# Finer waits in the feed-forward stage and a shorter way from the router into the experts

## The chip, the cores and the metric

The kernel runs on one core of a Trainium2 chip. The metric is the device time in microseconds (us) from the start to the end of one execution. The engines of the core are named as in its profile: PE is the matrix engine (PEld its weight loads), DVE the vector engine, ACT the scalar engine, POOL the GpSimd engine, SP the engine that issues most of the DMAs. Each works through its own list of instructions in order, and semaphores order them against each other.

## What is computed

The program is a stack of blocks over 512 tokens of width 1024, all in float32: a gated delta rule mixer, a SwiGLU feed-forward layer, a state space (S5) mixer, a mixture of experts and two attention layers, each with a residual and a layer norm. Two pieces matter here.

```python
def swiglu(x, w1, w3, w2):
    return (jax.nn.silu(x @ w1) * (x @ w3)) @ w2
...
    logits = (xt @ w_router).astype(jnp.float32) + b_router.astype(jnp.float32)
    top_v, top_i = lax.top_k(logits, TOP_K)
    gates = jax.nn.softmax(top_v, axis=-1)
    dense_gate = jnp.sum(jax.nn.one_hot(top_i, N_EXPERTS, dtype=jnp.float32) * gates[..., None], axis=1)
    y = jnp.zeros_like(xt)
    for e in range(N_EXPERTS):
        y = y + dense_gate[:, e:e + 1].astype(x.dtype) * swiglu(xt, w1[e], w3[e], w2[e])
```

The feed-forward layer has 2816 hidden features, the mixture eight experts (two per token) with 1408 each.

## The kernel before

**Three passes.** A float32 product is made of three products of rounded operands: high times high, low times high, high times low (`three_pass`). ACT writes the high part of a weight tile (`split_hi`, `ffn_w_hi`), DVE the low part as raw minus high (`split_lo`, `ffn_w_lo`), and only then may PE use it (`take`). The low part overwrites nothing that PE still reads: three tiles are held (`SPLITS`), and ACT waits with tile j until PE has entered tile j-2 (`tile_used`, `leave`).

**The feed-forward stage** (`dense_parts` with `beside` and `end` set) runs two parts of 1408 hidden features. A part has 18 tiles: 12 up tiles (six chunks, for each the w1 and the w3 tile, 1 MB each and 0.5 MB in the last chunk) and 6 down tiles. The eight PSUM banks serve the up products in a turn of four; then `keep_busy` (L194) puts six matmuls on a constant, then the down products accumulate in all eight banks. `keep_busy` computes nothing that is used. DVE multiplies gate and value (`ffn_prod`, L2710), POOL splits the product (`hid_hi`, `hid_lo`), and after the last down tile DVE adds the banks to `acc`.

**What runs beside it.** `Parameters` prepares later stages on DVE meanwhile. `condition` (L1896) multiplies two 128x1024 blocks of `ada_t` after each low part; SP loads two more blocks after each low part and before the next weight tile (`loads`, L1753). `output_powers` (L1879 to L1884) makes a group of powers, waits first for the store of the group before (L1769), and SP stores the group before it issues the next weight tile. In the first part the last two groups are computed one after the other, between the low parts of the second and the third down tile.

**The end of the stage.** The last three down tiles of the second part are gone through token block by token block (four of 128), with both halves of 512 columns in turn under each tile, so that `EndNorm` can add, measure (L2548), aggregate, centre and scale a block on DVE while PE does the next one. `turn` transposes the block.

**The router** (`router`, stage `s5_glu`) makes the layer norm, stores the rows of `x_tok` to DRAM, computes the logits, takes the two best experts, and counts with matrices of ones the place of each token within its expert (L3305) and the load of each expert (L3309). The flag `moe_fits` says whether all experts have at most 192 tokens.

**Into the experts** (`sparse_parts`). All engines load the flag and branch. SP loads the small table of slot numbers (L3159) and the first weight tiles (L2449). DVE compares the table with the places (`make_pick`), PE turns the picks into row numbers (`spots`, L2844), DVE reads them out (`read_spots`), POOL gathers the rows by an indirect DMA (L3052), PE transposes them (`turn`, L2852 and L2854), ACT and DVE write their high and low parts (`x_hi`, `x_lo`), and the first expert's up products begin (L2870). `keep_busy` stands three times in between:

```python
        keep_busy(prog, 6, 6)
        pe.wait_ge(token_ready, 1)
        spots(0)
        keep_busy(prog, 6, 12)
        turn(0)
        keep_busy(prog, 6, 4)
```

One `keep_busy` call is two records of PE in the trace. All eight experts then run in a loop.

## Time and profile before

| | |
|---|---|
| median of 3 runs | 2688.17 us (2687.33 to 2690.44) |
| profiled execution | 2686.12 us |
| its span, first to last instruction | 2684.4 us |
| mean granted clock of PE | 0.986 of full |
| PE busy | 2537.4 us, 95% |
| DVE, ACT, POOL busy | 64%, 38%, 20% |
| feed-forward stage in the trace | about 470 to 862 us |
| router and way into the experts | about 1060 to 1143 us |
| experts | about 1143 to 1780 us |

Times in the rows are from the start of the span. A busy PE can be a PE that works on `keep_busy`. An engine's idle time costs only where PE waits at its end.

### The profile page before, as it was taken

Reading aid. Unit: us, or ns where it says so; the run is one execution under the profiler, and the core shown is the slowest. Engines: PE = TensorE matmul, PEld = TensorE weight load, DVE = VectorE, ACT = ScalarE, POOL = GpSimd, SP = SyncE. Lnnn points to the kernel's source line nnn. Section 1 sums busy time; section 2 is a strip of 40 time slices with the busy share of each in tenths; the row PEclk is TensorE's granted clock in tenths of the full one; section 3 lists DMA queues with packets and bytes.
Section 4 is the critical chain, followed back from the end, with each engine's and each line's share of the span. In section 5 each row is a group of like instructions: output and inputs, shape, how many; then the busy total and the mean of one; then the engine's idle time right before and its main releaser. Section 6 shows DMA issues by size and latency. Waiting matters only on the chain. (4 is left out here: it accounts for less than half of the span.)

```text
span 2684.4 us, 42100 instructions
## 1 busy us (share of the span) xinstructions
PE 2537.4 (95%) x16443; PEld 2086.8 (78%) x16443; DVE 1720.3 (64%) x2855; ACT 1032.3 (38%) x1472; POOL 543.6 (20%) x429
## 2 busy tenths in 40 slices
PE   8998989999999989899999999989998989999897
PEld 7887887778877769799999999967675666776466
DVE  6745666466676783566666667665775546677456
ACT  3341213321212342355555555513343443344353
POOL 1104431430320110143233344320110001020001
PEclk9999999999999999999999999999999989999999
DMA  4221001346653342367777777743220212322021
GB/s 149 92 82 33 2 3 63 121 156 228 201 185 131 108 125 80 108 215 236 232 256 238 232 236 251 263 150 90 70 90 27 85 56 71 97 77 72 26 79 63
DMA packets 262242, 340.82 MB, mean 127 GB/s; under 512 B 24960, under 2 KB 220032, under 8 KB 261504
## 3 DMA queue, kind: packets, MB, share of 16 engines
q1 hardware_dynamic: 253888, 315.52, 36.6%
q0 software_dynamic: 4736, 16.78, 1.8%
q10 hardware_dynamic: 3456, 6.29, 0.8%
q8 instruction: 110, 1.80, 0.3%
q14 instruction: 52, 0.43, 0.1%
HBM read 318.63 MB, written 17.30 MB: 125 GB/s over the span
## 5 line engine op out<-in xcount | busy, mean ns | idle before, releaser
L2870 PE MATMUL ps<-x_feat_r,moe_w_hi 128*128 128x384 f32 x1408 | 405.1, 359 | 1.0 <-DVE x_feat_r L2970 1.0
L2476 DVE TENSOR_TENSOR moe_w_lo<-ring,moe_w_hi 128x2048 fp32r<-128x2048 f32 x144 | 314.5, 2184 | 117.7 <-ACT moe_w_hi L2471 117.5
L2873 PE MATMUL ps<-x_feat_r,moe_w_lo 128*128 128x192 f32 x1408 | 354.5, 252 | 0.0
L2471 ACT ACTIVATE moe_w_hi<-ring 128x2048 fp32r<-128x2048 f32 x144 | 255.0, 1771 | 99.3 <-PE ps L263 72.8
L2873 PEld LDWEIGHTS ps<-x_feat_r,moe_w_lo 128*128 128x128 f32 x1408 | 268.8, 191 | 0.3
L2870 PEld LDWEIGHTS ps<-x_feat_r,moe_w_hi 128*128 128x128 f32 x1408 | 264.2, 188 | 1.9 <-issue 1.6
L267 PE MATMUL ps<-x_free_r,ring_r 128*128 128x512 f32 x496 | 196.5, 396 | 0.0
L266 PE MATMUL ps<-ring_r,x_feat_r 128*128 128x256 f32 (+2 forms) x576 | 186.3, 323 | 0.0
L194 PE MATMUL ps<-cst 128*128 128x384 f32 x370 | 135.8, 519 | 19.6 <-PEq L175 17.3
L263 PE MATMUL ps<-x_feat_r,ffn_w_hi 128*128 128x512 f32 x352 | 139.3, 396 | 0.7 <-DVE ffn_w_lo L2476 0.7
L267 PE MATMUL ps<-x_feat_r,ffn_w_lo 128*128 128x512 f32 x352 | 139.4, 396 | 0.0
L266 PE MATMUL ps<-x_free_r,ffn_w_hi 128*128 128x512 f32 x352 | 138.5, 393 | 0.0
L2471 ACT ACTIVATE ffn_w_hi<-ring 128x2048 fp32r<-128x2048 f32 (+1 forms) x36 | 63.6, 1772 | 179.4 <-PE ps L263 136.0
L194 PEld LDWEIGHTS ps<-cst 128*128 128x128 f32 x370 | 72.1, 202 | 68.8 <-issue 30.8
L3778 ACT ACTIVATE s_sb<-s_sb,att_small 128x512 f32<-128x512 f32 (+3 forms) x128 | 71.8, 561 | 139.7 <-DVE att_small L3770 139.3
L266 PEld LDWEIGHTS ps<-ring_r,x_feat_r 128*128 128x128 f32 x576 | 110.8, 192 | 8.7 <-issue 0.6
L267 PEld LDWEIGHTS ps<-x_free_r,ring_r 128*128 128x128 f32 x496 | 93.6, 189 | 21.1
L3767 DVE CUSTOM_DVE_ANT_0 s_sb<-ps,tables 128x128 f32<-128x128 f32 (+3 forms) x104 | 49.3, 474 | 91.1 <-PE ps L3717 74.0
L3785 ACT ACTIVATE p_t<-ps 128x512 f32<-128x512 f32 (+3 forms) x128 | 55.0, 430 | 130.5 <-PE ps L3717 130.4
L263 PE MATMUL ps<-x_feat_r,acc_r 128*128 128x512 f32 x256 | 102.0, 398 | 0.0
L2917 ACT ACTIVATE moe_cross<-ps 128x384 f32<-128x384 f32 (+1 forms) x96 | 44.3, 462 | 146.8 <-PE ps L2873 146.8
L266 PE MATMUL ps<-x_free_r,acc_r 128*128 128x512 f32 x256 | 100.6, 393 | 0.0
(615 smaller groups left out, 6454.4 us busy)
## 6 DMA issues: line engine op xcount, KB each, us to landing
ring<-in_moe_w SPq DMA_DIRECT2D x120, 1024.0 KB, 5.5
ring<-in_w_in SPq DMA_DIRECT2D x32, 1024.0 KB, 5.3
ring<-in_ffn_w SPq DMA_DIRECT2D x30, 1024.0 KB, 7.0
ring<-in_ada_t SPq DMA_DIRECT2D x48, 512.0 KB, 4.1
ring<-in_gdn_w_in SPq DMA_DIRECT2D x12, 1024.0 KB, 5.7
ring<-in_moe_w SPq DMA_DIRECT2D x24, 512.0 KB, 3.8
ring<-in_s_w_glu SPq DMA_DIRECT2D x8, 1024.0 KB, 5.4
ring<-in_w_out SPq DMA_DIRECT2D x8, 1024.0 KB, 6.3
```

What stands on the lines that cost most here:

```text
L194: prog.nc.tensor.matmul(prog.ps[:, bank, 0:3 * P], prog.ident, prog.cst, start=True, stop=True)
L263: m = nc.tensor.matmul(out, lh, rh, start=first, stop=False)
L266: nc.tensor.matmul(out, lh, rl, start=False, stop=False)
L267: return nc.tensor.matmul(out, ll, rh, start=False, stop=last)
L2471: self.prog.nc.scalar.activation(self.flat(self.hi, j % SPLITS, j), self.raw(j), ACT.Copy).then_inc(self.hi_done, 1)
L2476: self.prog.nc.vector.tensor_tensor(self.flat(self.lo, j % SPLITS, j), self.raw(j), self.flat(self.hi, j % SPLITS, j).bitcast(F32), ALU.su ...
L2870: mm = nc.tensor.matmul(out, wh[:, k, cs], both[:, k, :], start=(k == 0), stop=False)
L2873: mm = nc.tensor.matmul(out[:, 0:SLOTS], wl[:, k, cs], xg[0][:, k, :], start=False, stop=(k == KD - 1))
L2917: nc.scalar.activation(cross_of(c, which), half(c, which, 1), ACT.Copy).then_inc(cross_copied, 1)
L3767: self.nc.vector.tensor_tensor_reduce(out=x, in0=scores, in1=table, scale=1.0, scalar=-3.0e38, op0=ALU.add, op1=ALU.max, accum_out=mx).the ...
L3778: self.nc.scalar.activation(x, x, ACT.Exp, bias=self.small[:, u % 4, 1:2], scale=self.heads[h][3], accum_out=self.small[:, u % 4, 2:3]).th ...
L3785: self.nc.scalar.activation(self.p_t[:, u % 2, 0:self.keys(u)], self.ps[:, 2 + u % 2, 0:self.keys(u)], ACT.Copy).then_inc(self.pt_copied, 1)
```

## The change

In the feed-forward stage: the first weight tile is rounded and split in four pieces, and PE waits for each piece of two k-steps rather than for the tile; `keep_busy` at the start goes from 8 to 2 calls. Between up and down the six `keep_busy` calls are gone, and the first down tile runs in an order of banks that follows when each comes free. The low part of the third down tile is computed between the two last groups of powers instead of behind both. In the token-by-token end each half of 512 columns is finished before the other begins, and its statistics are taken directly after its addition.

Between router and experts: the ranks are computed with four matmuls (32, 24, 16 and 8 columns) instead of ten, the loads with one instead of four, followed by one more reduction; the subtraction of 1 from the places is moved into the table. The slot table and the first three tiles of the first expert are loaded in the router stage (`first_expert_tiles`, after the stores of the rows); SP signals them in the expert stage. `keep_busy` before the spots goes from 6 to 2 calls. ACT rounds two tiles before the rows instead of one, DVE splits the first tile before `find_homes` and the second before the rows.

```diff
@@ class PartStream @@
+        self.first_hi, self.first_lo = None, None
+
+    def in_pieces(self, st):
+        self.first_hi, self.first_lo = st.counter("first_hi"), st.counter("first_lo")
+
+    def piece(self, p):
+        k, n = tile_rows(0)
+        return slice(p * k * n // PIECES, (p + 1) * k * n // PIECES)
+
+    def first_pieces_hi(self, act):
+        act.wait_ge(self.landed[0], 16)
+        act.wait_ge(self.tile_used, 1)
+        for p in range(PIECES):
+            cs = self.piece(p)
+            self.prog.nc.scalar.activation(self.hi[:, 0, cs], self.raw(0)[:, cs], ACT.Copy
+                                           ).then_inc(self.first_hi if p < PIECES - 1 else self.hi_done, 1)
+
+    def first_pieces_lo(self, dve):
+        for p in range(PIECES):
+            cs = self.piece(p)
+            if p < PIECES - 1:
+                dve.wait_ge(self.first_hi, p + 1)
+            else:
+                dve.wait_ge(self.hi_done, 1)
+            self.prog.nc.vector.tensor_tensor(self.lo[:, 0, cs], self.raw(0)[:, cs], self.hi[:, 0, cs].bitcast(F32), ALU.subtract
+                                              ).then_inc(self.first_lo if p < PIECES - 1 else self.lo_done, 1)
...
     def loads(self, sp):
 
         for j in range(RAW):
-            self.load(sp, 0, j)
+            sp.wait_ge(self.prog.expert_landed[j], 16)
+            sp.sem_inc(self.landed[j], 16)
...
+def first_expert_tiles(prog, sp, stage, inp):
+
+    W = prog.weights
+    for j in range(RAW):
+        c0, c1 = CHUNKS[j // 2]
+        src = inp[("moe_w1", "moe_w3")[j % 2]][0][0][:, c0:c1].rearrange("(k p) n -> p k n", p=P)
+        last_there = W.size[stage] - RING + j
+        sp.wait_ge(W.used, W.released[W.first[stage] + last_there])
+        sp.dma_start(W.ring[:, j, 0:KD * (c1 - c0)].rearrange("p (k n) -> p k n", n=c1 - c0), src
+                     ).then_inc(prog.expert_landed[j], 16)
...
@@ class EndNorm @@
-    def spread(self, dve, t, added, count):
+    def half_stats(self, dve, t, h, added, count):
+        dve.wait_ge(added, count)
+        self.nc.vector.bn_stats(self.stats[:, t, 6 * h:6 * h + 6], self.acc[:, t, h * BANK:(h + 1) * BANK]
+                                ).then_inc(self.measured, 1)
+
+    def spread(self, dve, t):
         self.link = self.link or linker(dve, self.norm_link)
-        dve.wait_ge(added, count)
-        for h in range(2):
-            m = self.nc.vector.bn_stats(self.stats[:, t, 6 * h:6 * h + 6], self.acc[:, t, h * BANK:(h + 1) * BANK])
-        self.link(m)
+        dve.wait_ge(self.measured, 2 * t + 2)
...
+FREED = (((5, 7), 0), ((0, 1, 2, 3), FT + 3), ((4, 6), FT + 4))
...
@@ dense_parts, tensor @@
         if beside:
-            keep_busy(prog, 7, 8)
+            keep_busy(prog, 7, 2)
...
                     for k in range(KD):
+                        if opening and m == 0 and k % (KD // PIECES) == 0:
+                            S_.first_piece(pe, k)
...
-            if beside:
-                keep_busy(prog, 5, 6)
-            pe.wait_ge(mult_done, e * FT + (FT + 4))
+            if not beside:
+                pe.wait_ge(mult_done, e * FT + (FT + 4))
...
                 wh, wl = S_.take(pe, e, j)
+                if beside and j == N_UP:
+                    pe.wait_ge(hid_ready, e * FT + 4)
+                    for banks, multiplied in FREED:
+                        if multiplied:
+                            pe.wait_ge(mult_done, e * FT + multiplied)
+                        for i in banks:
+                            t, cs = slice((i // 2) * P, (i // 2 + 1) * P), slice((i % 2) * BANK, (i % 2 + 1) * BANK)
+                            for m in range(2):
+                                three_pass(nc, ps[:, i, :], (hid_hi[:, m, t], hid_lo[:, m, t]), (wh[:, m, cs], wl[:, m, cs]),
+                                           m == 0, False, S_.leave if m == 0 and i == FREED[0][0][0] else None)
+                    continue
...
                 for t in range(NT):
-                    for j in range(N_TILES - by_token.TILES, N_TILES):
-                        if j not in held:
-                            held[j] = S_.take(pe, e, j)
-                        wh, wl = held[j]
-                        for r in range(tile_rows(j)[0]):
-                            m = 2 * (j - N_UP) + r
-                            pe.wait_ge(hid_ready, e * FT + (m + 3))
-                            for h in range(2):
-                                cs = slice(h * BANK, (h + 1) * BANK)
+                    for h in range(2):
+                        cs = slice(h * BANK, (h + 1) * BANK)
+                        for j in range(N_TILES - by_token.TILES, N_TILES):
+                            if j not in held:
+                                held[j] = S_.take(pe, e, j)
+                            wh, wl = held[j]
+                            for r in range(tile_rows(j)[0]):
+                                m = 2 * (j - N_UP) + r
+                                pe.wait_ge(hid_ready, e * FT + (m + 3))
...
@@ dense_parts, vector @@
                 if beside and c == LAST:
                     beside.vector(dve, e, LAST - 1)
-                    beside.vector(dve, e, LAST)
-            for j in range(N_UP + 2, N_TILES):
+            split_lo(e, N_UP + 2)
+            if beside:
+                beside.vector(dve, e, LAST)
+            for j in range(N_UP + 3, N_TILES):
                 split_lo(e, j)
...
@@ sparse_parts @@
-        keep_busy(prog, 6, 6)
+        keep_busy(prog, 6, 2)
         pe.wait_ge(token_ready, 1)
         spots(0)
         keep_busy(prog, 6, 12)
...
         S_.split_hi(act, 0, 0)
+        S_.split_hi(act, 0, 1)
         x_hi(0)
-        S_.split_hi(act, 0, 1)
...
-        dve.wait_ge(table_landed, 16)
+        dve.wait_ge(prog.slots_landed, 16)
         make_pick(0)
         nc.vector.tensor_copy(token.rearrange("p t n -> p (t n)"), token_id).then_inc(token_ready, 1)
         read_spots(0)
+        S_.split_lo(dve, 0, 0)
         low_gate = find_homes()
-        S_.split_lo(dve, 0, 0)
+        S_.split_lo(dve, 0, 1)
         x_lo(0)
-        S_.split_lo(dve, 0, 1)
...
@@ router @@
                 sp.dma_start(gb[:, :, :], inp["ln_gb"][2]).then_inc(landed, 16)
+                sp.dma_start(table, prog.slot_table).then_inc(prog.slots_landed, 16)
...
                 for t in range(NT):
                     sp.wait_ge(normed, t + 1)
                     sp.dma_start(prog.x_rows[t * P:(t + 1) * P, :], x_tok[:, t, :]).then_inc(stored, 16)
+                first_expert_tiles(prog, sp, "s5_glu", inp)
                 sp.wait_ge(stored, 16 * NT)
...
                 pe.wait_ge(chosen, 1)
-                for t in range(NT):
-                    for b in range(t + 1):
-                        m = nc.tensor.matmul(ps[:, 5, t * EXPERTS:(t + 1) * EXPERTS], prog.tri if b == t else prog.ones,
-                                             left[:, b, 0:EXPERTS], start=(b == 0), stop=(b == t))
+                nc.tensor.matmul(ps[:, 5, 0:NT * EXPERTS], prog.tri, left[:, :, 0:EXPERTS], start=True, stop=False)
+                for b in range(1, NT):
+                    m = nc.tensor.matmul(ps[:, 5, b * EXPERTS:NT * EXPERTS], prog.ones, left[:, 0:NT - b, 0:EXPERTS],
+                                         start=False, stop=(b == NT - 1))
                 m.then_inc(ranked, 1)
-                for t in range(NT):
-                    m = nc.tensor.matmul(ps[:, 7, 0:EXPERTS], prog.ones, left[:, t, 0:EXPERTS], start=(t == 0), stop=(t == NT - 1))
-                m.then_inc(ranked, 1)
+                nc.tensor.matmul(ps[:, 7, 0:NT * EXPERTS], prog.ones, left[:, :, 0:EXPERTS], start=True, stop=True
+                                 ).then_inc(ranked, 1)
...
-                dve.wait_ge(ranked, 2)
-                link(nc.vector.memset(place[:, :, EXPERTS:], -1.0))
-                pl = place[:, :, 0:EXPERTS]
-                link(nc.vector.tensor_tensor(pl, ps[:, 5, 0:NT * EXPERTS].rearrange("p (t n) -> p t n", n=EXPERTS),
-                                             left[:, :, 0:EXPERTS], ALU.mult))
-                link(nc.vector.tensor_scalar(pl, pl, 1.0, None, ALU.subtract))
-                link(nc.vector.tensor_reduce(den[:, 0:1], ps[:, 7, 0:EXPERTS], AX_X, ALU.max))
+                nc.vector.memset(place[:, :, EXPERTS:], 0.0)
+                dve.wait_ge(ranked, 1)
+                nc.vector.tensor_tensor(place[:, :, 0:EXPERTS], ps[:, 5, 0:NT * EXPERTS].rearrange("p (t n) -> p t n", n=EXPERTS),
+                                        left[:, :, 0:EXPERTS], ALU.mult)
+                dve.wait_ge(ranked, 2)
+                link(nc.vector.tensor_reduce(top[:, 0, 0:EXPERTS], ps[:, 7, 0:NT * EXPERTS].rearrange("p (t n) -> p n t", n=EXPERTS),
+                                             AX_X, ALU.add))
+                link(nc.vector.tensor_reduce(den[:, 0:1], top[:, 0, 0:EXPERTS], AX_X, ALU.max))
                 nc.vector.tensor_scalar(flag[:, :], den[:, 0:1], SLOTS + 0.5, None, ALU.is_lt)
```

`first_piece` is the wait of PE for one piece. In the constants, the slot numbers of the table go from 0, 1, ... to 1, 2, ..., and the first rows of the experts are one less. Both new sets of semaphores live outside the stages.

## Rows read from the trace of the kernel before

**Rows 1.** Windows: us, PE, PEld, DVE, ACT, POOL busy, granted clock, DMA share, GB/s

```profile
663.00:787.00 124.00, 124.00 (x535) 99.92 (x534) 85.43 (x94) 27.21 (x23) 36.49 (x20) 1.00 0.59 193
...
1143.00:1780.00 637.00, 633.66 (x3889) 588.50 (x3890) 427.89 (x370) 341.29 (x329) 230.64 (x179) 1.00 0.72 233
```

**Rows 2.** Waits of PE over the feed-forward stage: total us, times, longest

```profile
PE ps L263 <- DVE ffn_w_lo L2476: 0.7, 1, 0.7
```

**Rows 3.** Timeline of the stage's opening: start us, us, engine, line, out<-in, [idle before <- releaser]

```profile
469.91 5.40 PE L194 MATMUL ps<-cst 128*128 128x384 f32 x16 [0.55 <-PEq L175]
...
471.10 5.51 ACT L2471 ACTIVATE ffn_w_hi<-ring 128x2048 fp32r<-128x2048 f32 x3 [2.35 <-SPq L2766]
...
473.04 8.97 DVE L2476 TENSOR_TENSOR ffn_w_lo<-ring,ffn_w_hi 128x2048 fp32r<-128x2048 f32 x3 [3.46 <-ACT ffn_w_hi L2471]
...
475.99 0.50 PE L263 MATMUL ps<-x_feat_r,ffn_w_hi 128*128 128x512 f32 x1 [0.68 <-DVE ffn_w_lo L2476]
```

**Rows 4.** The low parts of the opening by source line: ns min/median/max

```profile
L2476 DVE TENSOR_TENSOR ffn_w_lo<-ring,ffn_w_hi x3: 2890/3119/3120, 473.0 to 478.9; 128x2048 fp32r<-128x2048 f32 x3
```

**Rows 5.** Window of the opening's gap, columns as in rows 1

```profile
475.00:476.00 1.00, 0.32 (x2) 0.01 (x1) 1.00 (x2) 1.00 (x1) 1.00 (x2) 1.00 0.00 0
```

**Rows 6.** Timeline of PE between up and down, first part

```profile
599.18 4.03 PE L194 MATMUL ps<-cst 128*128 128x384 f32 x12
602.76 0.68 PE L263 MATMUL ps<-ffn_w_hi,ffn_hid_hi 128*128 128x512 f32 x1
603.28 0.40 PE L266 MATMUL ps<-ffn_w_lo,ffn_hid_hi 128*128 128x512 f32 x1
```

**Rows 7.** Timeline of DVE in the first part's down phase

```profile
616.87 0.76 DVE L1879 TENSOR_TENSOR x_tok<-x_tok,s_pow 128x576 f32<-128x576 f32 x1 [3.71 <-DMA s_q<-x_tok]
...
621.26 2.29 DVE L2476 TENSOR_TENSOR ffn_w_lo<-ring,ffn_w_hi 128x2048 fp32r<-128x2048 f32 x1
...
625.75 2.29 DVE L2476 TENSOR_TENSOR ffn_w_lo<-ring,ffn_w_hi 128x2048 fp32r<-128x2048 f32 x1
```

**Rows 8.** Timeline of SP, the two blocks issued before the third down tile's successor

```profile
614.47 1.48 SPq L1753 DMA_DIRECT2D ring<-in_ada_t  x2
```

**Rows 9.** Those two blocks by tensor: time from issue to landing

```profile
DMA to landing us min/median/max: 7.0/7.8/8.7
```

**Rows 10.** Timelines of ACT and DVE, last down tile of the stage

```profile
825.20 1.06 ACT L2471 ACTIVATE ffn_w_hi<-ring 128x1024 fp32r<-128x1024 f32 x1 [9.27 <-PE ps L263]
...
826.30 1.23 DVE L2476 TENSOR_TENSOR ffn_w_lo<-ring,ffn_w_hi 128x1024 fp32r<-128x1024 f32 x1 [8.04 <-ACT ffn_w_hi L2471]
```

**Rows 11.** Timeline of DVE after the last down product

```profile
855.13 1.29 DVE L2548 BATCH_NORM_STATS2 ffn_stats<-acc 128x6 f32<-128x512 f32 x2
```

**Rows 12.** Timelines of PE, DVE and POOL from the ranks to the row transposes

```profile
1116.06 2.40 PE L3305 MATMUL ps<-moe_chosen,cst 128*128 128x8 f32 x20 [1.61 <-DVE moe_chosen L3393]
1118.31 1.21 PE L3309 MATMUL ps<-moe_chosen,cst 128*128 128x8 f32 x8
...
1120.33 0.15 DVE L3409 TENSOR_SCALAR moe_fits<-moe_den 128x1 int32<-128x1 f32 x1
...
1121.84 6.11 PE L194 MATMUL ps<-cst 128*128 128x384 f32 x12 [2.31 <-issue]
...
1124.07 1.01 DVE L2957 TENSOR_SCALAR moe_pick<-moe_table,moe_place 128x192 fp32r<-128x192 f32 x4 [3.58 <-DMA moe_table<-in_slot_table]
...
1127.49 1.03 PE L2844 MATMUL ps<-moe_token,moe_pick 128*128 128x2 f32 x8
...
1129.71 1.18 POOL L3052 DMA_INDIRECT moe_rows_in<-x_rows,moe_spot  x1 [180.41 <-DVE moe_spot L2964]
...
1137.59 1.09 PE L2852 MATMUL ps<-cst,moe_rows_in 128*128 128x128 f32 x8 [1.22 <-DMA moe_rows_in<-x_rows,moe_spot]
```

**Rows 13.** Windows at the ranks' end and in the first keep_busy, columns as above

```profile
1119.00:1119.50 0.50, 0.50 (x4) 0.43 (x3) 0.00 (x0) 0.00 (x0) 0.00 (x0) 0.53 0.00 0
...
1125.00:1126.00 1.00, 1.00 (x3) 0.50 (x2) 0.16 (x2) 0.00 (x0) 0.00 (x0) 0.57 0.70 183
```

More of the change, by code:

```diff
@@ L2400 @@
 SPLITS = 3
+PIECES = 4
 SLOTS = 192
@@ L2603, in tensor @@
                 c, which = divmod(j, 2)
-                wh, wl = S_.take(pe, e, j)
+                opening = beside and e == 0 and j == 0
+                if opening:
+                    wh, wl = S_.view(S_.hi, 0, 0), S_.view(S_.lo, 0, 0)
+                else:
+                    wh, wl = S_.take(pe, e, j)
                 if which == 0:
@@ L3119, in dense_ffn, with moe_experts @@
             st.gpsimd(gpsimd)
-def moe_experts(prog, name, w, gates, place, chosen, flag):
+def moe_experts(prog, name, w, gates, place, chosen, flag, table):
     nc = prog.nc
@@ L3166, in moe_experts, with router @@
             st.gpsimd(either(4))
-def router(prog, inp, gates, place, left, flag):
+def router(prog, inp, gates, place, left, flag, table):
     nc, ps, W = prog.nc, prog.ps, prog.weights
```

50 lines of the change are left out of this document (31 added, 19 removed).

## The prediction

> **What bounds the kernel now.** I read the windows by stage first. In them the matrix engine (PE) is busy for 124.0 of 124 us in the second part of the feed-forward stage and for 633.7 of 637 us in the experts [rows 1]. There only fewer PE instructions, or fewer gaps at the seams, can move the end. The other engines matter only where PE waits for them. The waits of PE over the feed-forward stage name a mere 0.7 us for the first low part `ffn_w_lo` [rows 2]. Not named are the `keep_busy` matmuls (L194), which count as busy but compute nothing. The change works at five seams, so I read the timeline at each. U is the moment when the last up matmul of a feed-forward part gives way, 599.18 us for the first part. One 512-column matmul takes 124/535 = 0.232 us (some records can be missing) [rows 1].
>
> **Part 1: opening of the feed-forward stage.** Before: ACT rounds the whole first tile from 471.10, DVE takes its low part from 473.04 for 2.89 us, PE starts at 475.99 [rows 3, 4]. After, both work in quarters. ACT does three whole tiles in 5.51 us, so a quarter of one is 0.46 us by share; with a fixed cost I take 0.60. DVE's quarter is 2.89/4 = 0.72, with a fixed cost 0.85. PE then starts at 471.10 + 0.60 + 0.85 + 0.10 of handovers = 472.65: 3.3 us earlier (bounds 3.0 and 3.6). It does not starve: a quarter is two of eight k-steps, 6 x 0.232 = 1.4 us, longer than DVE's 0.85. The cut from 8 to 2 `keep_busy` costs no time itself: 16 records took 5.40 us and would otherwise end at 475.3, behind the new start; two calls end at about 471.2. The gap of 1.4 us which this leaves is priced as a rival below; the gap of 0.68 in the old order left the clock at full rate [rows 5]. Tile 1 (low part ready by 478.5, wanted at 472.65 + 48 x 0.232 = 483.8) has 5 us of cover.
>
> **Part 2: the up-to-down seam, twice.** The 12 records of six `keep_busy` calls start at 599.18 and the first down matmul stands at 602.76, the next one 0.52 us later instead of 0.23 [rows 6]. So 3.58 + 0.29 = 3.87 us per seam, 7.7 us for both parts, as the second seam has the same shape. They are removed. Something must take their place: the down products want banks that the last up products still hold. The new order does banks 5 and 7 first (12 matmuls, 2.8 us), then 0 to 3 (24, 5.6 us), then 4 and 6. The last product `ffn_prod`, which frees 4 and 6, is done at U+0.9, against U+8.4 where it is wanted. `ffn_w_lo` of the first down tile was finished before U in both parts. I keep the whole 7.7 us; bounds 5.5 (part of it returned by the waits of part 3) and 7.7.
>
> **Part 3: the down tiles come 3.87 us sooner, can their low parts follow?** In the new clock PE wants the third down tile at U + 96 x 0.232 = U+22.3 and the fourth at U+33.4. Before, DVE started the low part of the third at 621.26, done at U+24.4 [rows 7]. That would now be 2.1 us late, and the change moves it ahead of the last group of powers: DVE is free of the group before at about U+14 (the six instructions of a group take 621.26 - 616.87 = 4.4 us, and the later group had waited 3.71 us for a store [rows 7]), so it ends at U+16.3, 6 us in hand. What is late next is the fourth. Behind the third's low part stand two `ada_t` blocks (`condition`), whose DMAs SP issues from 614.47 and which land 7.0 and 8.7 us later, so at U+22.3 and U+24.9 [rows 8, 9]. DVE, until now behind them, waits: blocks done at U+26.1, powers (4.4) at U+30.5, low part of the fourth (2.3 us as at 625.75 [rows 7]) at U+32.8. Wanted at U+33.4: 0.6 us in hand. SP queues the store of these powers and the load of the sixth down tile behind the same wait; the tile is issued at about U+31 instead of U+27.6 and wanted at U+55.7, covered. Cost 0 taken, bounds 0 and 2.1 (the lateness that the third tile would have had).
>
> **Part 4: end of the stage.** The last three tiles are taken by token, and now by half. The last tile is therefore wanted after 12 matmuls, 2.8 us, instead of 24. Its ACT rounding begins only when PE has entered the third last tile (825.20, entry at about 824.71), its low part runs 826.30 to 827.53 [rows 10]: 2.9 us after entry. PE waits 0.1 to 0.2 us, once. In return the first half of the last token block is complete 15 matmuls = 3.5 us before the second, so one addition and one of the two statistics of L2548 move under PE. The two take 1.29 us [rows 11]; one of them, 0.60 us, leaves the path (the addition of the first half was finished before the second half in the old order too). DVE is free for it: the previous block's chain has some 0.3 us left. Net +0.45, bounds 0 and 0.65.
>
> **Part 5: the router and the way into the experts.** The 20 + 8 rank records run from 1116.06 to 1119.52 [rows 12], 0.12 us each. Five matmuls in their place are 10 records, done at about 1117.5; DVE reaches its waits at 1117.3 anyway, then a product, two reductions and the flag: 0.8 us, so the flag is written at 1118.3 instead of 1120.48 [rows 12]. That is 2.2 us at the seam. PE entered the experts 1.36 us after the flag (1121.84), hence at 1119.6. DVE waited for the table until 1124.07; it now lies in SBUF, so `pick` starts at about 1120.1 and ends at 1121.2. Two `keep_busy` calls end by 1121.7, where six held the spots back until 1127.49 [rows 12]. At half clock I give the spots 2.1 us: read at 1123.8 instead of 1128.56. The gather, first issued at 1129.71, goes at 1124.9 and its second half 1.5 us later. Before, it landed at 1137.5, 6.3 us after the second issue, while three 1 MB tiles were coming in [rows 12]; those are now prefetched behind the last row store, at 1110, and gone by 1121. With 6.3 us it lands at 1132.7. On the other side stand 24 `keep_busy` records in front of the transposes. Here the clock decides. The granted clock fell to half (1.2 GHz) at 1119.0 although PE was 100% busy with rank matmuls of 8 columns (0.53 of full over 1119.0 to 1119.5), and came back to 2.4 GHz at 1125.9 (0.57 over the us before 1126), after `keep_busy` had run since 1121.84 [rows 12, 13]. So tiny matmuls did not hold it, and the spots will not raise it. If it stays low for h us after the spots, the 24 records end at 1123.8 + 24 x 0.32 + h/2. I take h = 4 as in the row: 1133.5, 4.1 us before 1137.59. Bounds: h = 6.9, the whole low stretch of before, gives 2.6; the gather alone as the limit gives 4.9, and a gather unhindered by the tiles with full clock 6.0. I take 4.1. From there to the first expert matmul the chain is the same; the low parts of two tiles, one of which stood behind it, are done by 1131.
>
> The Trainium skill (TensorE: Matmul & The Clock Gate, Part 1) says that the array runs at half rate by default and gets the full rate only after sustained work, and advises against idle gaps. This speaks against dropping `keep_busy` calls; the trace agrees that idle or nearly idle stretches cost the clock, and at the up-to-down seam there is no gap left for it to act on. By that rule alone the opening of part 1 would lose what the first rival gives.
>
> **Sum.** 3.3 + 7.7 + 0 + 0.45 + 4.1 = 15.6 us. The profiled execution took 2686.12 us (span 2684.4), so 2670.6; the median of the runs shown is 2.05 us above it, so 2672.6. Low bound of the gains: 3.0 + 5.5 + 0 + 2.6 = 11.1; high: 3.6 + 7.7 + 0.65 + 6.0 = 18.0.
>
> **Rivals.**
> - A, the clock drops in the 1.4 us gap of the opening. For it: only two `keep_busy` calls, and tiny work before. Against: in the slice from 475 PE was busy 0.32 us and the clock stayed at 1.00 [rows 5]. A low stretch of 4 us as at 1121.84 costs 4/2 = 2.0 us: total 2674.6.
> - B, the fourth down tile's low part is late. It decides once the blocks land more than 0.6 us later than before. Landings of 7.0 to 8.7 us spread by 1.7, so the price is up to 1.1 us, with the bound of 2.1 above: 2673.7 to 2674.7.
> - C, the way into the experts gives nothing beyond the 2.2 us of the ranks, because the gather or the `keep_busy` behind the spots ends as late, relative to the flag, as before: 2674.5.
> - D, given back: DVE, behind `condition`, keeps the down phase as long as before in part one (3.87 lost) and A and C hold too: 2680.4.
> - E, slower: the experts start in another phase between ACT, DVE and PE, and in their loop PE begins to wait per expert. At 15.6/8 = 2.0 us per expert the gain is gone, from 21.0/8 = 2.6 it is measurably slower; 2.7 would give 2672.6 + 21.6 = 2694.2. Against it: PE is 99.5% busy over all eight [rows 1], no instruction of the loop changes, and the loop settles from tile to tile.
> - F, no effect: the removed `keep_busy` only uncover waits as long as themselves, and the start of the gather is set by something older: within 5 us of 2688.
>
> **How the numbers follow.** A measurement of this kernel tells about 0.2% from no change, 5.4 us. Forecast 0.48, A 0.13, B 0.14, C 0.12, D 0.06, E 0.03, F 0.04. The first five are faster by more than 5.4 us: 0.93; F is same, 0.04; E slower, 0.03. The range from 2668.5 to 2679.0 takes in the high bound of the gains (2670.2) with the runs' own spread of 1 to 2 us, and the low bound (2677.1) with the same; D, E and F, 0.13 in all, stay out.
>
> **What would show it.** Right: first feed-forward matmul about 1.55 us after ACT's first rounding instead of 4.9; no L194 record between up and down, and the stage from that first matmul to the last down matmul 7.5 us shorter; no PE wait for `ffn_w_lo` in the down tiles; one L2548 instead of two in the last chain; flag to `turn` in about 15.2 us instead of 17.1, rank records 10. Wrong: PE waits for `ffn_w_lo` of the fourth down tile (B), granted clock under 1 in the opening (A), a DMA wait in front of the row transposes that ends as long after the flag as before (C), waits per expert (E).

## The result, and the profile after

The changed kernel took 2675.39 us at the median of five runs (2670.87 to 2676.81), the kernel before beside it 2690.44 (2687.33 to 2693.04). The ratio is 0.9936, with a 95% interval of 0.9924 to 0.9949, so by the ratio the gain is 17.2 us (13.7 to 20.4); the two medians lie 15.05 us apart. Timed once more it gave 2676.39 and 0.9937 (0.9923 to 0.9951). The forecast was 2672.6 and a gain of 15.6. The profiled execution took 2675.39 us with a span of 2673.7: only 10.7 us shorter than the profiled execution before, which was itself 4.3 us under the median of the runs before (2686.12 against 2690.44). Where these 10.7 come from follows from seven points that exist in both traces: A, ACT's first rounding of the feed-forward stage; M, the first up matmul; S, the first ACT instruction of the stage behind it (L1950 in both kernels); R, the first rank matmul; F, the flag; E, the first expert matmul; G and H, the first scatter behind the experts and the last transpose (L557) of the attention after it.

| stretch | before, us | after, us | gain | predicted |
|---|---|---|---|---|
| A to M, opening | 4.89 | 1.50 | 3.39 | 3.3 |
| M to S, seams, down tiles, end of stage | 395.74 | 387.74 | 8.00 | 8.15 |
| S to R, four stages, where the change adds only loads on SP | 244.33 | 245.04 | -0.7 | 0 |
| R to F, ranks | 4.27 | 2.80 | 1.47 | 2.2 |
| F to E, way into the experts | 22.76 | 22.03 | 0.73 | 1.9 |
| E to G, experts | 639.6 | 639.8 | -0.2 | 0 |
| G to H, attention | 466.5 | 469.1 | -2.6 | 0 |

The start of A (0.4 us earlier) and the end behind H (0.2) make up the rest. Flag means the start of the instruction that writes `moe_fits`. The feed-forward stage gave 11.4 of 11.45 us; the way from the router into the experts gave 2.2 of 4.1; stages that run the same instructions as before took 3.5 back. All these terms compare one execution of each kernel.

The timelines of the changed kernel at the opening, at the first up-to-down seam, in DVE's down phase and behind the last down product, columns as in [rows 3]:

```profile
469.50 1.53 PE L194 MATMUL ps<-cst 128*128 128x384 f32 x4 [0.55 <-PEq L175]
...
470.69 2.19 ACT L2444 ACTIVATE ffn_w_hi<-ring 128x512 fp32r<-128x512 f32 x4 [2.35 <-SPq L2844]
...
471.35 2.73 DVE L2454 TENSOR_TENSOR ffn_w_lo<-ring,ffn_w_hi 128x512 fp32r<-128x512 f32 x3 [2.17 <-ACT ffn_w_hi L2444]
472.19 0.47 PE L263 MATMUL ps<-x_feat_r,ffn_w_hi 128*128 128x512 f32 x1 [1.17 <-DVE ffn_w_lo L2454]
...
595.12 0.40 PE L267 MATMUL ps<-x_feat_r,ffn_w_lo 128*128 128x512 f32 x1
595.35 0.39 PE L263 MATMUL ps<-ffn_w_hi,ffn_hid_hi 128*128 128x512 f32 x1
...
609.25 2.29 DVE L2511 TENSOR_TENSOR ffn_w_lo<-ring,ffn_w_hi 128x2048 fp32r<-128x2048 f32 x1
617.33 1.23 DVE L1896 SCALAR_TENSOR_TENSOR ring<-ring,x_tok 128x1024 f32<-128x1024 f32 x1 [5.79 <-DMA ring<-in_ada_t]
...
624.12 2.28 DVE L2511 TENSOR_TENSOR ffn_w_lo<-ring,ffn_w_hi 128x2048 fp32r<-128x2048 f32 x1
...
843.57 0.69 DVE L2594 BATCH_NORM_STATS2 ffn_stats<-acc 128x6 f32<-128x512 f32 x1
```

PE begins 1.50 us after the start of ACT's first quarter instead of 4.89 after the start of the whole tile [rows 3]. At 595.35 a down matmul takes its regular 0.39 us directly behind the last up matmul, where twelve L194 records stood [rows 6]. The third down tile's low part now starts 13.9 us after that seam; then DVE waits 5.79 us for the blocks of `condition`, and the fourth low part ends at 626.4, 31.05 us after the seam, where 33.4 is wanted. One statistics instruction stands in the last chain instead of two [rows 11]. Over the stage the view of PE's waits has nothing for a down tile's `ffn_w_lo`.

The same view from the ranks to the first expert matmul, to be laid beside [rows 12]:

```profile
1104.97 0.64 PE L3378 MATMUL ps<-moe_chosen,cst 128*128 128x32 f32 x2 [1.61 <-DVE moe_chosen L3467]
...
1105.41 1.43 PE L3380 MATMUL ps<-moe_chosen,cst 128*128 128x24 f32 x6
...
1106.69 0.61 PE L3383 MATMUL ps<-moe_chosen,cst 128*128 128x32 f32 x2
...
1107.77 0.15 DVE L3484 TENSOR_SCALAR moe_fits<-moe_den 128x1 int32<-128x1 f32 x1
...
1111.43 1.85 PE L2920 MATMUL ps<-moe_token,moe_pick 128*128 128x2 f32 x8
1113.14 10.65 PE L194 MATMUL ps<-cst 128*128 128x384 f32 x24
...
1113.46 2.27 DVE L2511 TENSOR_TENSOR moe_w_lo<-ring,moe_w_hi 128x2048 fp32r<-128x2048 f32 x1
1114.46 2.44 POOL L3128 DMA_INDIRECT moe_rows_in<-x_rows,moe_spot  x1 [177.40 <-DVE moe_spot L3040]
...
1117.20 0.91 POOL L3128 DMA_INDIRECT moe_rows_in<-x_rows,moe_spot  x1 [0.30 <-issue]
...
1124.30 1.09 PE L2928 MATMUL ps<-cst,moe_rows_in 128*128 128x128 f32 x8 [0.51 <-DMA moe_rows_in<-x_rows,moe_spot]
```

Windows of the same stretch, columns as in [rows 1]:

```profile
1105.00:1110.00 5.00, 3.02 (x11) 2.67 (x12) 1.56 (x10) 0.27 (x2) 0.00 (x0) 0.50 0.95 330
1110.00:1115.00 5.00, 5.00 (x15) 3.30 (x14) 2.67 (x8) 3.71 (x2) 0.54 (x1) 0.50 0.01 3
1115.00:1118.00 3.00, 3.00 (x6) 1.58 (x5) 2.66 (x12) 0.00 (x0) 2.70 (x2) 0.50 0.18 33
1118.00:1119.00 1.00, 1.00 (x3) 0.55 (x3) 0.97 (x4) 0.00 (x0) 0.93 (x2) 0.73 1.00 329
```

Three things differ from the forecast. The clock was at half from the ranks to 1118.5, so the ten rank records took 0.21 us each instead of 0.12, and the 24 `keep_busy` records behind the spots 10.65 us. POOL's first gather issue took 2.44 us instead of 1.18, beside DVE's low part of the first expert tile, which the change had moved there. The rows landed 7.1 us after the second issue, although the queues had been nearly empty (DMA share 0.01 from 1110 to 1115); the 1 MB load of the next tile had been issued at 1116.0, 1.2 us ahead of it.

### The profile page after: what moved, and what is told of

Its sections match the earlier page's. It is cut to its first block and busy times, and to the rows that moved or that the text cites. A ratio compares the mean times of both kernels' runs of the same rounds, so it can differ in the third digit from the quotient of the medians.

```text
span 2673.7 us, 41986 instructions
## 1 busy us (share of the span) xinstructions
PE 2526.5 (94%) x16381; PEld 2079.4 (78%) x16381; DVE 1721.1 (64%) x2858; ACT 1032.3 (39%) x1475; POOL 545.4 (20%) x429
## 5 line engine op out<-in xcount | busy, mean ns | idle before, releaser
L194 PE MATMUL ps<-cst 128*128 128x384 f32 x326 | 125.8, 538 | 21.0 <-PEq L175 19.0
L194 PEld LDWEIGHTS ps<-cst 128*128 128x128 f32 x326 | 65.6, 209 | 66.2 <-issue 34.8
L267 PE MATMUL ps<-x_feat_r,ring_r 128*128 128x512 f32 x256 | 101.1, 395 | 0.0
```

Of the source, the lines that this page charges most:

```text
L194: prog.nc.tensor.matmul(prog.ps[:, bank, 0:3 * P], prog.ident, prog.cst, start=True, stop=True)
L267: return nc.tensor.matmul(out, ll, rh, start=False, stop=last)
```

## Experiments

The tables below use the points A to H of each run's own trace; single whole times are not used for effects under 4 us, since A alone lay between 470.7 and 474.5 in these traces, before anything that was edited.

**One half of the change at a time.** `ffn_only` keeps the hunks of `PartStream`, `dense_parts` and the norm at its end; `entry_only` keeps those of `router`, `sparse_parts`, `moe_experts` and the table:

```diff
# ffn_only, against the kernel before
-            keep_busy(prog, 7, 8)
+            keep_busy(prog, 7, 2)
...
-            if beside:
-                keep_busy(prog, 5, 6)
# entry_only, against the kernel before
+                first_expert_tiles(prog, sp, "s5_glu", inp)
...
-        keep_busy(prog, 6, 6)
+        keep_busy(prog, 6, 2)
```

> The kernel before with only the edits of the feed-forward stage (opening in quarters, no keep_busy between up and down with the new order of banks, third down tile's low part ahead of the last powers, last token block by half); router and way into the experts as before. The changed kernel's profile shows the end of the feed-forward stage 12.2 us earlier, of which the clock at the last transposes gives some 0.8. Theory 1 (the stage's gain is its own and passes through to the end): 11.5 to 12.5 us earlier at the stage's last transposes, and 10 to 12 us at the end of the kernel, ratio about 0.9959. Theory 2 (what is gained before is given back in stages whose clock falls in another phase, in the stretch from 850 to 975 us and in the first attention, about 2.5 us in the changed kernel): 8.5 to 10 us at the end. Theory 3 (the gain of the stage needs the entry's edits): under 8.

> The kernel before with only the edits of the router and of the way into the experts; feed-forward stage as before. Prediction's terms: flag 2.2 us earlier and entry 1.9 more, 4.1 us, ratio 0.9985. Theory now, from the changed kernel's trace: flag 1.5 us earlier, from flag to the row transposes 0.7 less, 2.2 in all, ratio 0.9992. What tells them apart is the distance from the first rank matmul to the first expert matmul: 27.0 us before, 24.8 in the changed kernel, 22.9 by the prediction. If the small gain is an accident of the clock's phase that the earlier start brought, it would be nearer 22.9 here; if it is the edits' own, 24.8 again.

`ffn_only`: 2685.13 us, ratio 0.9977 (0.9966 to 0.9987), a gain of 6.2. `entry_only`: 2686.41 us, 0.9984 (0.9975 to 0.9992), 4.3. Together 10.5, less than the 17.2 of both; the intervals (3.5 to 9.1 and 2.0 to 6.7 us against 13.7 to 20.4) leave little room for a plain sum. From A to S `ffn_only` took 389.85 us against 400.6 before: the stage's gain is its own. But from R to E it took 31.6 against 27.0, in code that it shares with the kernel before. Its timeline and windows:

```profile
1109.09 4.43 PE L3368 MATMUL ps<-moe_chosen,cst 128*128 128x8 f32 x20 [1.61 <-DVE moe_chosen L3456]
1113.38 1.85 PE L3372 MATMUL ps<-moe_chosen,cst 128*128 128x8 f32 x8
```

```profile
1108.00:1113.00 5.00, 3.91 (x19) 3.91 (x19) 1.71 (x15) 1.38 (x5) 0.00 (x0) 0.59 0.00 0
1113.00:1118.00 5.00, 2.67 (x12) 2.58 (x12) 0.76 (x5) 0.00 (x0) 0.00 (x0) 0.50 0.00 0
```

Here the clock fell ahead of the ranks and not at their end [rows 13], and the same 28 records took 6.1 us instead of 3.5 [rows 12]. The size of the gain is that of theory 3, but not for its reason: the stage gave 10.8 us without the other edits, and in this trace the old entry took 4.6 of them back. 2.7 of these lie before the flag, at half clock; 1.2 lie in the rows, which landed 7.5 us after the second gather issue instead of 6.3, with no edit there. The twelve times of `ffn_only` fall in two groups: three from 2675.6 to 2679.4 at a mean granted clock of 0.986, nine from 2683.4 to 2691.8 at 0.980 to 0.984. The profiled execution (2686.16) is one of the nine, so the other three may have lost nothing at the entry; no trace of them exists. `entry_only` had 24.8 us from R to E, as the changed kernel, although its ranks ran at full clock; so 2.2 us is the edits' own size against the profiled execution before, and not an accident. At full clock the ranks gave 2.5 us (1.76 from R to F instead of 4.27), and from F to E `entry_only` took 23.0 us against 22.8 before: all of its gain is that of the ranks. Its timed gain of 4.3 us cannot tell 2.2 from the predicted 4.1, since its interval holds both. The old entry's price was 27.0 in one trace and 31.6 in the other; the new one stayed between 24.0 and 25.1 in the seven traces that have it (one of them without the prefetch). That can be why both halves together gain more than their sum; how often the old entry is the dear one, no run here shows.

**The third down tile's low part.**

```diff
-            split_lo(e, N_UP + 2)
-            if beside:
-                beside.vector(dve, e, LAST)
-            for j in range(N_UP + 3, N_TILES):
+                    beside.vector(dve, e, LAST)
+            for j in range(N_UP + 2, N_TILES):
```

> The changed kernel with the third down tile's low part back behind the last group of powers. Prediction: PE wants it 22.3 us after the last up matmul gives way, and it would be ready at about 24.4: a wait of 2.1 us for ffn_w_lo in part one, the same or less in part two, so 2 to 4 us. Rival: with the seam gone DVE's blocks also move forward and the wait shrinks to under 0.5 us, so that this edit is worth nothing.

From A to S 392.9 us instead of 389.2. The waits and windows of PE in this run:

```profile
PE ps L263 <- DVE ffn_w_lo L2511: 2.2, 1, 2.2
```

```profile
620.00:622.00 2.00, 0.98 (x3) 0.77 (x4) 2.00 (x2) 0.06 (x1) 0.00 (x0) 0.82 0.93 383
622.00:624.00 2.00, 2.00 (x7) 1.51 (x6) 2.00 (x5) 0.93 (x1) 0.00 (x0) 0.50 0.49 117
```

The wait of 2.2 us is the predicted 2.1, in part one only. Behind the gap the clock was at half for 3.4 us; the other 1.5 us fit that. The run's whole time was 2674.72 us, like the changed kernel's: 2.7 us less from S to R (242.4) and 1.0 less from G to H (468.1), in code that is the same, hid the loss.

**The opening and the seam.**

```diff
# kb_opening0
-            keep_busy(prog, 7, 2)
# kb_updown
-            if not beside:
-                pe.wait_ge(mult_done, e * FT + (FT + 4))
+            if beside:
+                keep_busy(prog, 5, 6)
+            pe.wait_ge(mult_done, e * FT + (FT + 4))
```

> The changed kernel without its last two keep_busy calls at the opening of the feed-forward stage (nothing of the computation is left out). The changed kernel has 1.17 us of idle PE before its first up matmul and kept the clock at 1.00. Here the idle stretch in front of it grows to about 3.5 us. Theory 1 (idle of this length costs the clock, rival A of the prediction): granted clock 0.50 for 3 to 5 us behind the first up matmul, and from that matmul to the first down matmul 125 us instead of 123.2. Theory 2 (the prediction's: the dense work before and after carries it): clock 1.00 and 123.2 us.

> The changed kernel with the six keep_busy calls and the wait for the last product back between the up and down matmuls of both parts; the new order of banks stays. Prediction: 3.87 us per seam, 3.5 of them between the last up matmul and the first down matmul, so 7 to 7.7 us in all from the first up matmul of the stage to its last transposes. Rival (PE was ahead of the low parts or the store anyway, so the seam only moves an idle stretch): under 5 us.

`kb_opening0` (2673.78 us): the first up matmul still comes 1.5 us after A, but from there to the first down matmul 124.7 us instead of 123.2. Its PE timeline and a window, and the same window of the changed kernel:

```profile
472.42 0.47 PE L263 MATMUL ps<-x_feat_r,ffn_w_hi 128*128 128x512 f32 x1 [3.24 <-DVE ffn_w_lo L2454]
```

```profile
472.00:476.00 4.00, 3.58 (x11) 2.91 (x12) 3.97 (x5) 4.00 (x5) 4.00 (x3) 0.71 0.12 25
```

```profile
472.00:476.00 4.00, 3.81 (x17) 3.12 (x18) 3.97 (x5) 4.00 (x4) 4.00 (x3) 1.00 0.10 21
```

Behind an idle stretch of 3.24 us the clock was at half for 3.4 us; behind one of 1.17 it stayed at 1.00, in all eleven traces that have the opening in quarters and the two calls. Rival A names a real mechanism, and the two calls left in place keep it away. Theory 1 holds in this one execution with a price of 1.5. `kb_updown` (2680.81 us): from M to S 395.4 us instead of 387.7, a difference of 7.7, the predicted value.

**The way into the experts.** Four edits to the changed kernel:

```diff
# no_prefetch
-                first_expert_tiles(prog, sp, "s5_glu", inp)
...
-            sp.wait_ge(self.prog.expert_landed[j], 16)
-            sp.sem_inc(self.landed[j], 16)
+            self.load(sp, 0, j)
# kb_spots6
-        keep_busy(prog, 6, 2)
+        keep_busy(prog, 6, 6)
# lo_behind, lo_behind_timed
-        S_.split_lo(dve, 0, 0)
         low_gate = find_homes()
+        S_.split_lo(dve, 0, 0)
         S_.split_lo(dve, 0, 1)
# clock_up_lo: lo_behind, and in the router
+                keep_busy(prog, 0, 2)
                 pe.wait_ge(chosen, 1)
...
                                  ).then_inc(ranked, 1)
+                keep_busy(prog, 0, 4)
```

> The changed kernel with the first three expert tiles loaded when the expert stage opens, as before, and not behind the router's last row store. Theory 1 (three tiles of 1 MB each beside the gather slow it): the rows land 1 to 2 us later after their second issue than the 7.1 us of the changed kernel, and the low part ahead of the search for the homes stands behind a tile that is not there yet. Theory 2 (the gather's time after its issue is its own and the queues' load does not matter): within 0.5 us of 7.1, and the first expert matmul moves by under 1 us.

> The changed kernel with six keep_busy calls in front of the spots again instead of two. Prediction: these calls held the spots back once the table no longer did. Theory 1: 12 records at half clock take 8 us, so the spots come 5 to 6 us later and all of it arrives at the first expert matmul, because neither gather nor keep_busy behind the spots can shrink: from the first rank matmul to the first expert matmul 29 to 31 us instead of 24.8. Theory 2: the longer dense stretch brings the clock back before the spots, so the 24 records behind them run at full rate and 2.6 us return: 26 to 28 us.

> The changed kernel with DVE's low part of the first expert tile behind the search for the homes again, as before the change. Theory 1 (this subtraction stands beside the Pool engine's writing of descriptors for the first gather, 2.44 us instead of 1.18, and is what slows it): first gather issue back at 1.2 us, landing 1.2 us earlier, but the 24 keep_busy records in front of the row transposes end only 0.5 us before the landing, so at most 0.5 us of it is kept. Theory 2 (the gather's issue is slow for another reason, the clock or the prefetch): issue stays at 2.4 us, and nothing changes up to the transposes. In both the low part moves behind the homes and ends before the first expert matmul wants it.

> The changed kernel with the low part of the first expert tile behind the search for the homes, as run once before; now timed. There it was 20.8 us from the first rank matmul to the first expert matmul instead of 24.8, with the first gather issue at 1.19 us instead of 2.44. Theory 1 (low part beside the descriptors is the cause): 20.8 again, and 3 to 4 us less than the changed kernel at the median. Theory 2 (it was the earlier return of the clock in that execution, 2.7 us on the 24 records): between 21 and 24, and 1 to 2 us at the median.

> The changed kernel with two edits: DVE's low part of the first expert tile goes behind the search for the homes again, and PE gets two keep_busy calls ahead of the wait for the chosen experts and four behind the rank matmuls, into bank 0, where the router has only idle time (nothing is left out). Theory (the entry is long because the clock falls in the router's idle stretches and because the low part stands beside the writing of the gather's descriptors): rank matmuls and spots at full clock, from the first rank matmul to the first expert matmul 20 us or less instead of 24.8, and 2666 to 2671 us at the end. Rival (keep_busy raises nothing, since it falls in gaps again after the flag): 20.8 us as with the low part moved alone, which was 4 us shorter than in the changed kernel. If the clock falls later instead, in the first expert's transposes, nothing is gained over that either.

"24 records" are those of `keep_busy` between spots and transposes, "landing" the time from the second gather issue until its rows are there. An asterisk marks the runs in which the transposes did not wait for the rows:

| run | first issue | next tile load against second issue | landing | 24 records | R to E | whole, us |
|---|---|---|---|---|---|---|
| changed | 2.44 | 1.2 before | 7.1 | 10.65 | 24.8 | 2675.39 |
| after_again | 2.44 | 1.2 before | 7.4 | 7.99 | 24.8 | 2676.39 |
| third_late | 2.43 | 1.2 before | 7.3 | 10.63 | 24.0 | 2674.72 |
| kb_spots6 | 2.43 | 1.2 before | 7.1 | 7.99 | 29.7 | 2682.94 |
| no_prefetch | 1.18 | three tiles, 4.3 to 5.4 before | 7.1* | 10.71 | 24.9 | 2672.35 |
| lo_behind | 1.19 | 2.7 behind | 4.5* | 7.99 | 20.8 | 2671.69 |
| lo_behind_timed | 1.19 | 2.7 behind | 4.6* | 10.69 | 24.1 | 2675.46 |
| clock_up_lo | 1.19 | 2.7 behind | 4.4* | 7.99 | 21.0 | 2671.51 |

In `after_again` the 24 records ended early, and PE waited for the rows all the same. These are its timeline, and that of `lo_behind_timed`:

```profile
1113.23 7.99 PE L194 MATMUL ps<-cst 128*128 128x384 f32 x24
...
1114.55 2.44 POOL L3128 DMA_INDIRECT moe_rows_in<-x_rows,moe_spot  x1 [176.44 <-DVE moe_spot L3040]
...
1124.70 1.09 PE L2928 MATMUL ps<-cst,moe_rows_in 128*128 128x128 f32 x8 [3.48 <-DMA moe_rows_in<-x_rows,moe_spot]
```

```profile
1116.16 10.69 PE L194 MATMUL ps<-cst 128*128 128x384 f32 x24
...
1117.49 1.19 POOL L3128 DMA_INDIRECT moe_rows_in<-x_rows,moe_spot  x1 [175.91 <-DVE moe_spot L3040]
...
1126.69 1.04 PE L2928 MATMUL ps<-cst,moe_rows_in 128*128 128x128 f32 x8
```

So two ends of the same length stand behind the spots. One is the gather, when the first tile's low part runs beside its descriptors: its first issue is 1.25 us longer, and the finished low part frees a slot, so that SP loads the next 1 MB tile 1.2 us before the second issue goes out (landing 7.1 to 7.4 us). `no_prefetch` separates the two: its first issue took 1.18 us with no low part beside it, and its rows landed as late all the same, behind three tile loads. The times from issue to landing of both gather halves, `no_prefetch` and then `lo_behind`:

```profile
DMA to landing us min/median/max: 7.1/7.1/7.2
```

```profile
DMA to landing us min/median/max: 4.5/4.7/4.8
```

Over all fourteen traces the rows landed 6.3 to 8.1 us after the second issue where loads of weight tiles had been issued ahead of it (ten traces), and 4.4 to 4.6 us where the next load came behind it (four). So the landing goes with the order of the load and the gather, and the length of the issue with the low part; no run moved the load alone. The other end is the 24 records at half clock. Take away only one and nothing moves (`after_again` had the fast records, `lo_behind_timed` the fast gather); without both, R to E is 20.8. `lo_behind` gave far more than either theory had, because both ends were short in it, the records by chance. `lo_behind_timed` missed both theories too: the issue is 1.19, but R to E 24.1 and the median unchanged (ratio 0.9942, 0.9928 to 0.9956). `no_prefetch` was within 0.5 us of 7.1 and moved the first expert matmul by 0.1, as theory 2 had it, but not for its reason: the load of the queues does matter, and the 7.1 of the changed kernel already holds it. The prefetch as placed gave nothing between R and E (24.9); there the records at half clock had the end, 0.7 us behind the rows. `kb_spots6` costs 4.9 us, as theory 1's lower end, although its clock came back before the spots: then the gather is the end. `clock_up_lo` kept the clock at 1.00 throughout, but its four calls ended 2 us behind the flag and held the stage's end, so R to E was 21.0: the rival's number, not its reason. Its ratio is 0.9931 (0.9917 to 0.9945).

**The changed kernel again, and a better one.** `after_again` is the changed kernel unedited.

```diff
# best, against lo_behind
+                keep_busy(prog, 0, 2)
                 pe.wait_ge(chosen, 1)
...
                                  ).then_inc(ranked, 1)
+                keep_busy(prog, 0, 1)
...
-        keep_busy(prog, 6, 12)
+        keep_busy(prog, 6, 10)
```

> The changed kernel itself once more, timed beside the two that follow on one chip. Prediction 2672.6 us; 2675.39 measured in five runs. If the profiled run's give-backs in later stages (clock fallen at the stage of s5 outputs and in the first attention) are what chance lays where and not the change's own, the same stretches show other granted clocks in this profile, and the median of more runs lies nearer 2673; if they are the change's own, they stand at the same places again and the median stays at 2675.

> The changed kernel with three edits: the low part behind the search for the homes; two keep_busy calls ahead of the wait for the chosen experts and only one behind the ranks (four of them ended 2 us after the flag and held the stage's end back by 1.6 us); ten calls instead of twelve behind the spots, where they and not the gather had the end. Theory: flag 1.7 us after the first rank matmul, spots 3.4 after the flag, transposes 12.5 after it or less: 19 to 19.7 us from ranks to the first expert matmul, a median 4 to 6 us below the changed kernel. Rival: one call is too little, the clock falls behind the flag, 20.5 to 21.5 us.

`after_again`: 2676.39 us (2673.99 to 2677.40). From S to R 244.8, from G to H 469.2: the expectation's second case, with the same cost at the same places. `best`: 2669.94 us (2666.02 to 2675.09), ratio 0.9918 (0.9902 to 0.9933), R to E 20.0 instead of 24.8. Its timeline:

```profile
1108.50 0.15 DVE L3486 TENSOR_SCALAR moe_fits<-moe_den 128x1 int32<-128x1 f32 x1
...
1113.78 6.70 PE L194 MATMUL ps<-cst 128*128 128x384 f32 x20
1115.10 1.18 POOL L3128 DMA_INDIRECT moe_rows_in<-x_rows,moe_spot  x1 [175.73 <-DVE moe_spot L3040]
1116.58 0.91 POOL L3128 DMA_INDIRECT moe_rows_in<-x_rows,moe_spot  x1 [0.30 <-issue]
...
1121.23 1.09 PE L2928 MATMUL ps<-cst,moe_rows_in 128*128 128x128 f32 x8 [0.76 <-DMA moe_rows_in<-x_rows,moe_spot]
```

The transposes start 4.65 us after the second issue, as the rows land. The clock still fell behind the flag, for 3.4 us, so 20.0 lies between theory and rival. The medians lie 6.45 us apart, above the expected 4 to 6. The means of the timed runs differ by 5.4 us (2675.7 and 2670.3; standard error 1.7 from the two spreads), so `best` beats both kernels, though it is not shown how much of it each of the three edits gives.

## Why the prediction was right, and where it was not

The time lay in the range and 2.8 us above the value. The kernel before also measured 2.3 us more beside it than at the start (2690.44 against 2688.17). By the ratio the gain was 1.6 us larger than forecast, with an interval that holds the forecast; by the two medians it was 0.5 smaller. In the traces the edited stretches gave 13.6 us of the 15.6 (3.39, 8.00, 1.47 and 0.73), and unedited ones took 3.5 of them back. No term accounts for the 17.2 of the ratio, and 13.6 lies at the low end of its interval: that the whole came out so near the forecast, although part 5 gave half of its term, is partly luck.

- **Part 1** held: 3.39 us against 3.3. The clock stayed up because of the two calls (`kb_opening0`).
- **Part 2** held: `kb_updown` gives 7.7.
- **Part 3** held, and the edit is worth more than its bound of 2.1 us: 3.7 (`third_late`), since the missing cost is that of the clock behind the wait. The fourth low part had 2.4 us in hand, not 0.6: the last block of `condition` was there at 618.6, 23.2 us after the seam, and not at 24.9. Rival B fell.
- **Part 4** was within what the table can tell: 8.00 for parts 2 to 4 against 8.15; no run took out the order by half alone, so its 0.45 is not shown by itself. The last transposes did start with a clock of 1.00, but the fall then came some 1.5 us later behind them and took that back.
- **Part 5** is where a term was mis-sized: 2.2 us against 4.1, under its low bound of 2.6. The ranks gave 1.47 instead of 2.2, because the ten records were priced at 0.12 us each, at full clock, and the clock fell with the first of them (0.50 from 1105); in `entry_only`, at full clock, they gave 2.5. In the entry the step that failed is "With 6.3 us it lands at 1132.7", with the second half of the gather issued 1.5 us behind the first. From flag to transposes it was 16.4 us, where the prediction wanted 15.2. The part named the moved low part only as work done in time. It did not ask what runs on POOL beside it, nor what its end releases: SP's next tile. By the runs this is 1.25 us of issue and some 2.5 us of landing. The term for the records, "I take h = 4", was too small as well (the clock stayed low for 5.2 us behind the spots, within the bound of 6.9), and either error alone was enough to hold R to E at 24 to 25.
- Rival C named this mechanism, and in the profile the truth (0.73 beyond the ranks) lies nearer to it than to the forecast. D, E and F fell: the down phase was not held, E to G is 639.8 against 639.6.
- What no part had is that stages without any edit move by more than the terms under dispute. G to H was 469.1 and 469.2 in the two profiles of the changed kernel, 465.7 to 466.5 in seven variants with the same attention code, and 467.5 to 469.8 in the other four; S to R lay between 242.3 and 245.2 over all fourteen. In all fourteen PE stands idle for 2.7 us some 276 us behind G. In the six traces with 467.5 or more the clock falls to half behind this gap, for 3.4 us; in the eight others it does not. Whether the changed kernel tends to the dear side there, two profiles cannot settle; it stays open.

## What to carry to other kernels

When work is moved forward on an engine that is off the path, ask what its end releases as well as what it waits for: here a low part finished early let a 1 MB load start ahead of a gather on which PE waited. Where a transfer and a `keep_busy` stretch end together, measure them together, for neither alone shows a gain. Read an effect of 1 to 4 us between two points of the trace next to the edit, since the whole time of one run can hide it.

## What was not expected of the hardware

The same instructions ran at different clocks in different executions. The windows of the kernel before and of `entry_only` over the same instructions of a stage ahead of the router, which neither changes:

```profile
1010.00:1013.00 3.00, 3.00 (x16) 3.00 (x16) 2.14 (x2) 1.33 (x1) 0.00 (x0) 0.50 0.64 244
```

```profile
1014.00:1017.00 3.00, 3.00 (x28) 3.00 (x27) 2.12 (x2) 1.18 (x1) 0.00 (x0) 1.00 0.71 263
```

At the lower of the two levels PE did 16 matmuls in 3 us, at the higher 28, and from S to R the two executions differ by 2.0 us (244.3 and 242.3). Idle stretches of 0.68 and 1.17 us in front of dense work left the clock at 1.00; those of 2.25 (`third_late`) and 3.24 us (`kb_opening0`) were followed by 3.4 us at 0.50, at some 1.5 us each. This agrees with the Trainium skill (TensorE: Matmul & The Clock Gate, Part 1), which warns of idle gaps, though of longer ones than these.

A fall can also miss a gap in one execution and meet it in the next. The gap behind G in the changed kernel and in `no_prefetch`, whose code is the same there, and the windows behind it:

```profile
2047.13 0.80 PE L3784 MATMUL ps<-kc,qc 64*128 64x128 f32 x4 [2.73 <-DVE s_sb L3838]
```

```profile
2047.00:2050.00 3.00, 2.87 (x7) 1.25 (x8) 2.07 (x12) 2.10 (x6) 0.00 (x0) 0.50 0.10 17
```

```profile
2045.44 0.49 PE L3782 MATMUL ps<-kc,qc 64*128 64x128 f32 x4 [2.72 <-DVE s_sb L3836]
```

```profile
2045.30:2048.30 3.00, 2.85 (x10) 1.18 (x11) 2.08 (x12) 2.09 (x6) 0.00 (x0) 1.00 0.11 18
```

So one trace with the clock lost behind a gap, as `third_late` or `kb_opening0`, shows that the gap can cost it and not that it does so each time.

A POOL gather issue of 1.18 us took 2.43 to 2.44 in each of the seven executions where a DVE subtraction of two SBUF tiles ran beside it, and 1.18 to 1.19 in the seven without. The times fit an issue that stands still until DVE is through: in the changed kernel DVE ends at 1113.46 + 2.27 = 1115.73, and 1.18 behind that is 1116.91, where the issue ends at 1114.46 + 2.44 = 1116.90; in the other six the two agree to 0.02 us. The Trainium skill (SBUF — State Buffer, Who interferes with whom) says that a tensor_tensor with both inputs in SBUF contends with GpSimd's reads and that the later of the two blocks fully. The trace agrees, for a gather that reads its list of rows from SBUF. The prediction had not weighed this rule.
